# Score planes by level for the four chunks of a head, copied under constant masks, in the mixer of a two-layer encoder trunk

## The reference

```python
def chunk_gated_linear_attention(q, k, v, log_g):
    '''Per head: S_t = diag(exp(log_g_t)) S_{t-1} + k_t v_t^T,  o_t = S_t^T q_t.'''
    ...
    a_diag = jnp.einsum('bhcitsd,bhcisd->bhcits', q[..., :, None, :] * decay_diag, k)
    ...
    a_off = jnp.einsum('bhcitjd,bhcjsd->bhcitjs', qo, ko) * before[:, None, :, None]
    a_full = (a_off + a_diag[..., :, :, None, :] * eye).reshape(B, H, NC, CHUNK, CHUNK)
    o_intra = jnp.einsum('bhcts,bhcsv->bhctv', a_full, vc)
    ...
    o_inter = jnp.einsum('bhctd,bhcdv->bhctv', qc * jnp.exp(bc), s_prev)
    o = (o_intra + o_inter).transpose(0, 2, 3, 1, 4).reshape(B, T, H, DV)
```

## Time and profile before

| | |
|---|---|
| median of 3 runs | 1338.24 us (1330.84 to 1340.97) |
| profiled execution | 1322.33 us |
| its span, first to last instruction | 1320.6 us |
| PE busy | 1258.5 us (95%) |
| DVE busy | 719.9 us (55%) |
| ACT busy | 521.7 us (40%) |
| mean granted clock of TensorE | 0.984 |

### The profile page before, as it was taken

How to read it: one execution, slowest core, us unless ns; L and a number is a source line. 1 busy time by engine, 2 the same in 40 slices (tenths; PEclk the granted TensorE clock), 3 DMA queues, 4 the chain that set the end, 5 groups by cost and what they waited for, 6 DMA issues and landing times.

```text
span 1320.6 us, 16222 instructions
## 1 busy us (share of the span) xinstructions
PE 1258.5 (95%) x5981; PEld 1015.6 (77%) x5981; DVE 719.9 (55%) x1054; ACT 521.7 (40%) x1003; POOL 103.2 (8%) x108
## 2 busy tenths in 40 slices
PE   5899999888999999999999999999999999999997
PEld 3678787676798888888888786656798888888886
DVE  6558888877565344443447246563554343443444
ACT  4543544442553232242435673331553232332332
POOL 2221112210055000000000000000000000000000
PEclk7999999989999999999999999999999999999999
DMA  4321121111433332323222232000332322333321
GB/s 115 105 72 48 33 65 49 53 44 49 159 105 108 95 100 96 96 95 95 96 96 81 64 84 69 32 33 16 96 96 96 96 96 97 96 101 99 100 82 64
DMA packets 94866, 107.96 MB, mean 82 GB/s; under 512 B 15281, under 2 KB 56338, under 8 KB 94802
## 3 DMA queue, kind: packets, MB, share of 16 engines
q1 hardware_dynamic: 93618, 102.64, 25.1%
q0 software_dynamic: 1184, 4.46, 1.0%
HBM read 104.98 MB, written 2.10 MB: 81 GB/s over the span
## 4 chain that ended last, share of the span: by engine, by line
PE 86%; DVE 6%; ACT 4%; issue 2%; DMA 1%; POOL 0%; DVEq 0%; SPq 0%; ACTq 0%
PE bank L1339 24%; PE bank L1341 24%; PE bank L1340 24%; PE pp L1461 2%; PE pp L1705 1%; PE pp L1704 1%; PE po L1722 1%; DVE tmp L1120 1%; DVE a_sb L1123 1%; PE pp L1378 1%; PE pp L1458 1%; ACT w_hi L445 1%; PE pp L1340 0%; PE pp L1341 0%; PE pp L1339 0%
## 5 line engine op out<-in xcount | busy, mean ns | idle before, releaser
L1339 PE MATMUL bank<-h_lo,w_hi 128*128 128x512 f32 (+3 forms) x568 | 221.3, 390 | 9.7 <-DVE h_lo L984 5.8
L1340 PE MATMUL bank<-h_hi,w_lo 128*128 128x512 f32 (+3 forms) x568 | 217.9, 384 | 0.0
L1341 PE MATMUL bank<-h_hi,w_hi 128*128 128x512 f32 (+3 forms) x568 | 217.8, 383 | 0.0
L1339 PEld LDWEIGHTS bank<-h_lo,w_hi 128*128 128x128 f32 (+1 forms) x568 | 107.0, 188 | 35.6 <-issue 15.2
L1339 PE MATMUL bank<-wx,a_hi 128*128 128x512 f32 x320 | 126.7, 396 | 5.3 <-DVE wx L455 5.3
L1203 DVE TENSOR_TENSOR tmp<-sq,bank 128x512 f32<-128x512 f32 x64 | 44.0, 688 | 156.3 <-ACT sq L838 156.3
L1341 PE MATMUL bank<-wx,a_hi 128*128 128x512 f32 x320 | 125.2, 391 | 0.0
L1340 PE MATMUL bank<-wx,a_lo 128*128 128x512 f32 x320 | 125.2, 391 | 0.0
L1341 PEld LDWEIGHTS bank<-h_hi,w_hi 128*128 128x128 f32 (+1 forms) x568 | 107.1, 189 | 21.6 <-issue 0.6
L1340 PEld LDWEIGHTS bank<-h_hi,w_lo 128*128 128x128 f32 (+1 forms) x568 | 107.2, 189 | 20.7 <-issue 1.0
L1339 PE MATMUL bank<-w_lo,a_hi 128*128 128x512 f32 x304 | 119.9, 394 | 2.6 <-DVE a_lo L1099 1.4
(11 more groups left out here) (277 smaller groups left out, 2124.3 us busy)
## 6 DMA issues: line engine op xcount, KB each, us to landing
stage<-in_mlp_w SPq DMA_DIRECT2D x128, 512.0 KB, 3.6
stage<-in_ev_w_in SPq DMA_DIRECT2D x28, 512.0 KB, 3.7
stage<-in_ev_w_out SPq DMA_DIRECT2D x8, 512.0 KB, 3.6
stage<-in_od_w_out SPq DMA_DIRECT2D x8, 512.0 KB, 3.5
stage<-in_od_w_in SPq DMA_DIRECT2D x10, 256.0 KB, 3.0
x_tok<-in_x SPq DMA_DIRECT2D x4, 512.0 KB, 5.3
gbc<-in_norm_gains POOLq DMA_DIRECT2D x4, 512.0 KB, 4.1
xr<-in_x POOLq DMA_DIRECT2D x1, 2048.0 KB, 9.2
```

Source lines behind the costliest of these rows:

```text
L1339: nc.tensor.matmul(dst, wh, xl_, start=first, stop=False)
L1340: nc.tensor.matmul(dst, wl, xh, start=False, stop=False)
L1341: return nc.tensor.matmul(dst, wh, xh, start=False, stop=last)
```

## The change

A head's work is now cut by plane and not by chunk. `STEPS` makes four steps of a head: planes 0 and 1, 2 and 3, 4 and 5, and 6. For each plane PE writes the scores of all four chunks side by side into one bank of 512 columns, in a ring of four banks (`planes`). DVE copies each plane under its mask (`copy_predicated`: where the mask is not zero the element is written, elsewhere the target keeps what it has) into the head's score buffer for all four chunks, one of two (`a_bufs`: all of `a_sb`, and half of `tmp`). The masks are disjoint and the same for every head, so the buffers are cleared once, and each head overwrites the same elements. The mask of plane 0 was all ones, over a region that was zero but for its blocks; it now is one on the blocks of levels 0 and 1 alone. The four outputs of a head are issued together, two long slots after its last step. The slots themselves, and the number of steps in each, stay as they were.

```diff
+STEPS = [(0, 1), (2, 3), (4, 5), (6,)]
...
-            pending = [pending[1], groups]
+            pending = [pending[1], [(o, c) for o, step in groups if step == len(STEPS) - 1 for c in range(NT)]]
...
+        planes, a_bufs = quad, [a_sb[:, :, :], tmp[:, 0, :].rearrange("p (c t) -> p c t", c=NT)]
...
-            ch.link(nc.gpsimd.memset(masks[:, 0, :], 1.0))
+            for r, c in ((slice(0, 64), slice(64, 128)), (slice(0, 32), slice(32, 64)), (slice(64, 96), slice(96, 128))):
+                ch.link(nc.gpsimd.memset(masks[r, 0, c], 1.0))
...
-            for b in range(2):
-                nc.vector.memset(pp[b][:, 0, :], 0.0).then_inc(p_zero, 1)
+            nc.vector.memset(pp[0][:, 0:4, :], 0.0).then_inc(p_zero, 1)
...
-            def group(o, c):
-                idx = o * NT + c
-                pm = tmp[:, :, :].rearrange("p a t -> p (a t)")[:, 0:PAIRS * P]
-                dve.wait_ge(p_done, idx + 1)
-                if idx >= 1:
-                    dve.wait_ge(a_ready, idx)
-                nc.vector.tensor_tensor(pm, pp[idx % 2][:, 0:PAIRS, :].rearrange("p l t -> p (l t)"),
-                                        masks[:, :, :].rearrange("p l t -> p (l t)"), ALU.mult).then_inc(p_read, 1)
-                dve.wait_ge(p_read, idx + 1)
-                nc.vector.tensor_reduce(a_sb[:, idx % 4, :], pm.rearrange("p (l t) -> p t l", l=PAIRS),
-                                        AX_X, ALU.add).then_inc(a_ready, 1)
-                if c == 2 and FIRST[PACK_OF[o]] == o:
+            def group(o, step):
+                a = a_bufs[o % 2]
+                if step == 0 and o < 2:
+                    nc.vector.memset(a, 0.0).then_inc(a_zero, 1)
+                    dve.wait_ge(a_zero, o + 1)
+                elif step == 0:
+                    dve.wait_ge(o_done, o - 1)
+                for plane in STEPS[step]:
+                    n = o * PAIRS + plane
+                    dve.wait_ge(p_done, n + 1)
+                    if plane:
+                        dve.wait_ge(a_ready, n)
+                    mask = masks[:, plane:plane + 1, :].to_broadcast([P, NT, P])
+                    nc.vector.copy_predicated(a, mask.bitcast(I32), planes[n % 4]).then_inc(a_ready, 1)
+                if step == 2 and FIRST[PACK_OF[o]] == o:
                     update_state(PACK_OF[o])
...
+            def pairs(o, step):
+                p, r = PACK_OF[o], head_rows(o)
+                if step == 0:
+                    pe.wait_ge(xl_ready, (p + 1) * (LEVELS + 2))
+                for plane in STEPS[step]:
+                    n = o * PAIRS + plane
+                    if n == 0:
+                        pe.wait_ge(p_zero, 1)
+                    elif n >= 4:
+                        pe.wait_ge(a_ready, n - 3)
+                    for c in range(NT):
+                        dst, s = planes[n % 4][:, c, :], slice(c * P, (c + 1) * P)
+                        if plane == 0:
+                            ...
+                        elif plane < PAIRS - 1:
+                            x_ = xls[p % 2][r, plane + 1, s]
+                            ins = nc.tensor.matmul(dst, x_, x_, start=True, stop=True)
+                        else:
+                            ins = nc.tensor.matmul(dst, ks[p % 3][r, s], qs[p % 3][r, s], start=True, stop=True)
+                    ins.then_inc(p_done, 1)
...
-                pe.wait_ge(a_ready, idx + 1)
-                ins = nc.tensor.matmul(po[:, s], vbuf[:, o % 4, s], a_sb[:, idx % 4, :], start=True, stop=(c == 0))
+                pe.wait_ge(a_ready, (o + 1) * PAIRS)
+                ins = nc.tensor.matmul(po[:, s], vbuf[:, o % 4, s], a_bufs[o % 2][:, c, :], start=True, stop=(c == 0))
```

More of the change, by code:

```diff
@@ L593, in load_gain @@
                 pool.dma_start(gbc[:, :], norm_gains[layer, n].partition_broadcast(P)).then_inc(gbc_in, 16)
-            pool.wait_ge(a_ready, 8 * NT)
+            pool.wait_ge(a_ready, 8 * PAIRS)
             load_gain(0)
@@ L731, in evacuate @@
                 if what in ("q", "k") and i >= 3:
-                    act.wait_ge(p_done, NT * FIRST[i - 2])
+                    act.wait_ge(p_done, PAIRS * FIRST[i - 2])
                 if what == "f":
@@ L1030, in decayed @@
                 if lv == 0 and p >= 2:
-                    dve.wait_ge(p_done, NT * FIRST[p - 1])
+                    dve.wait_ge(p_done, PAIRS * FIRST[p - 1])
                 dve.wait_ge(e_ready, done + 2 if lv <= LEVELS else done + 1)
@@ L1407, in out_head @@
                     if idx == 0:
-                        pe.wait_ge(p_read, 8 * NT - 1) if j == 0 else pe.wait_ge(prob_exp, 4 * MLA_HEADS)
+                        pe.wait_ge(a_ready, 8 * PAIRS) if j == 0 else pe.wait_ge(prob_exp, 4 * MLA_HEADS)
                 if t == 0 or idx == KD - 1:
@@ L1446, in head_rows @@
                 return slice(first, first + w_)
-            def pairs(o, c):
-                p, idx, r, s = PACK_OF[o], o * NT + c, head_rows(o), slice(c * P, (c + 1) * P)
-                pe.wait_ge(xl_ready, (p + 1) * (LEVELS + 2))
-                if idx >= 2:
-                    pe.wait_ge(p_read, idx - 1)
-                else:
-                    pe.wait_ge(p_zero, idx + 1)
-                for lv in range(2):
-                    L = 64 >> lv
-                    for b in range(0, P, 2 * L):
-                        nc.tensor.matmul(pp[idx % 2][b:b + L, 0, b + L:b + 2 * L], xls[p % 2][r, lv, c * P + b:c * P + b + L],
-                                         xls[p % 2][r, lv, c * P + b + L:c * P + b + 2 * L], start=True, stop=True)
-                for lv in range(2, LEVELS):
-                    nc.tensor.matmul(pp[idx % 2][:, lv - 1, :], xls[p % 2][r, lv, s], xls[p % 2][r, lv, s],
-                                     start=True, stop=True)
-                nc.tensor.matmul(pp[idx % 2][:, PAIRS - 1, :], ks[p % 3][r, s], qs[p % 3][r, s], start=True,
-                                 stop=True).then_inc(p_done, 1)
+            def pairs(o, step):
[11 more added lines that the diff above has]
+                        if plane == 0:
+                            for lv in range(2):
+                                L = 64 >> lv
+                                for b in range(0, P, 2 * L):
+                                    left = xls[p % 2][r, lv, c * P + b:c * P + b + L]
+                                    right = xls[p % 2][r, lv, c * P + b + L:c * P + b + 2 * L]
+                                    ins = nc.tensor.matmul(dst[b:b + L, b + L:b + 2 * L], left, right, start=True, stop=True)
+                        elif plane < PAIRS - 1:
[4 more added lines that the diff above has]
+                    ins.then_inc(p_done, 1)
@@ L1466, in outputs @@
             def outputs(o, c):
-                p, idx, r, s = PACK_OF[o], o * NT + c, head_rows(o), slice(c * P, (c + 1) * P)
+                p, r, s = PACK_OF[o], head_rows(o), slice(c * P, (c + 1) * P)
                 if c == 0:
```

2 lines of the change are left out of this document (1 added, 1 removed).

## The result

| | before | after |
|---|---|---|
| median, runs of this comparison | 1334.54 us (1323.12 to 1340.97, 4 runs) | 1312.39 us (1305.08 to 1314.34, 4 runs) |
| profiled execution, its span | 1322.33, 1320.6 us | 1312.53, 1310.8 us |
| mean granted clock in it | 0.984 | 0.980 |
| PE, DVE busy | 1258.5, 719.9 us | 1259.0, 672.9 us |

The ratio measured is 0.9865, 95% interval 0.9822 to 0.9909: faster by a little over 1%, where 1324 us, 1.1% less, was forecast. The medians of four runs above are 22 us apart, but the four runs before lie 18 us from end to end. So the difference came out as forecast.

The account below looks back on a forecast made before the run. TensorE was taken to bound the kernel, mixer edits counting through its idle time and clock. 12.7 us of idle time plus 1.7 us of clock, 14.4 us off the 1338.24 us median, gave 1324 us; range 1311 to 1340 us.

Parts of the forecast that it names:

- PE sets the end, and only its gaps count: Whole kernel: TensorE is the bound; a mixer edit is worth its change in PE's idle time (22.0 us) and clock.
- Work taken off DVE is worth nothing by itself: Mixer: VectorE loses 52 us of 202, but this alone was to bring no time.
- comes from where the outputs stand: Mixer: most of the 14.4 us gain was credited to the outputs' new place, not to VectorE's relief.
- five gaps at outputs: PE waits of 1.80, 4.01, 1.04, 2.52 and 1.70 us in the mixer, all to go by issuing outputs later.
- Rival 1: Mixer: VectorE's lateness is behind all gaps; all 21.65 us and clock falls go, 25.4 us, 1313 us; chance 0.12.
- ScalarE's chain: Ahead of key transposes and chunk states: rinv work without idle time, 6.73 us from clamp to rinv; it was to stay.
- the 2.21 us that should have stayed: PE's gap at 215.03 us: chunk states wait for rinv on ScalarE, nothing of DVE in it; no gain claimed.
- rival 2: Mixer: gaps move, half of 12.7 us returns as waits for rinv or misc; 6 us less, 1332 us; chance 0.15.
- I cost this at nothing: TensorE's score matmuls: same number and shapes in another order, 0 us but for the clock.
- The fall at 300 us: Granted clock of 0.72 in 298 to 304 us after the 4.01 us gap; was to go with it, 1.7 us.
- rival 3: Runs of plane 0: four to eight clock falls of 1.7 us give back 7 to 14 us, 1331 to 1338 us; chance 0.12.
- Nothing in the trace to tell why: Base: the median of 1338.24 us stood 15.9 us above the profiled execution, unexplained; the gain was taken from the median.

Follow-up runs that it names:

- e8: Kernel before with VectorE's load taken down: sum over masked planes left out, one 128x128 copy in its place; 1312.86 us, ratio 0.9898.
- e1: Kernel before with only the four outputs of a head issued together, two slots after its last group; 1324.55 us, ratio 0.998.
- e2: Changed kernel with 72 further VectorE minima of 128x512 behind its copies, so VectorE's load is as before; 1327.51 us, ratio 1.0008.
- e9: Kernel before with a head's outputs issued together and the sum over masked planes replaced by one copy; 1313.14 us, ratio 0.9905.
- e5: The changed kernel measured again, unaltered, on another chip against the kernel before; 1311.34 us, ratio 0.9876.
- second batch: Runs on one chip of the kernel before (11 runs, median 1325.77 us) together with e5 to e8.
- e7: Changed kernel with ScalarE's rinv steps first in their slot and plane 0's small matmuls sorted by tile shape; 1290.49 us, ratio 0.9722.
- e6: Changed kernel with ScalarE's two rinv steps moved ahead of the evacuation, decays and cast in their slot; 1299.76 us, ratio 0.9789.
- e4: Changed kernel with plane 0's small matmuls sorted by shape, halves of all four chunks first, then quarters; 1302.27 us, ratio 0.9805.

## Why the prediction came out, and where its steps failed

- **Right: PE sets the end, and only its gaps count.** 383 to 700 us has 317.00 us of PE again.
- **Failed: "Work taken off DVE is worth nothing by itself", and with it that most of the gain "comes from where the outputs stand".** The relief alone is worth 12.9 us (e8), the place alone 0.3 us (e1), and with DVE's load put back nothing is left (e2). Each of the five gaps at outputs had been put down to position ("whatever DVE's speed"), since PE stood there one slot after DVE was given the work. But DVE was up to a whole slot late (8.6 us at the chunk states above), and its lateness made these gaps: four of them go and the fifth falls from 4.01 to 1.04 us when DVE alone is relieved. Rival 1 had the mechanism right for all but ScalarE's chain.
- **The gaps: right where named, but two were missed.** The 6.08 and 0.69 us and the outputs without any came as forecast; the 2.21 us that should have stayed became 2.61. I followed state to the outputs and not to the other reader of `misc`, though the order shows the sum of squares waiting for `state_ready`: 1.64 us, and 1.45 us behind it. Idle time fell by 9.2 and not by 12.7 us; that much of rival 2 came.
- **Mis-sized: TensorE's order, "I cost this at nothing".** By plane, the small matmuls follow each other and the large too, 0.2 to 0.4 us a head in the rows above, 2 to 3 us for eight. e9, which has the relief and the place but the old order, has a product of span and clock of 1289.4, the changed kernel 1285.4 us. That is 4 us, by medians from two batches, and no more than an indication by itself.
- **The clock: wrong in its places, near in sum, and not for the reason given.** The fall at 300 us stayed, with a gap still ahead of it. New ones came at 136 and 163 us with no gap ahead (rival 3's kind), both while PE was in the scores of a head with 64 rows, begun at 132.45 and 160.14; and one at 214.5, at the gap of 2.61 us, where the 2.21 us before had brought none. The places are not fixed: e5, the same kernel, has no fall at 136. In the profiled execution (1 - 0.980) x 1310.8 = 26.2 us are lost against (1 - 0.984) x 1320.6 = 21.1 us. By the medians of the second batch it is no loss but a gain: 0.979 before, 0.981 after, where 1.7 us were forecast and (1 - 0.979) x 1324.0 - (1 - 0.981) x 1309.6 = 2.9 us came, by the median spans. That figure is good to 2 or 3 us at best, since the median clock of the kernel before went from 0.977 to 0.980 between batches. So the forecast's 1.7 us came near for no reason that it gave.
- **The base.** "Nothing in the trace to tell why" the median stood 15.9 us above the profiled execution: in the second batch the runs before had times up to 1336.96 us, clocks of 0.970 to 0.982, and products of 1294.2 to 1298.2 us. The clock differs from run to run, the work hardly does. The profiled execution, at 0.984, was a good one. Over all 57 runs of the kernel before its median is 1326.8 us, over ten runs of the changed one 1312.3: the 1338.24 us of three runs was some 11 us high, and by itself put the forecast of 1324 us that much too high.
- **The sizes.** The copy took 735 ns, 0.69 forecast; DVE in the window 158 us and not 150: 2.5 us of this is the copies, and the rest goes with PE being further on at 331 us, the low part of head 6 at 319.69 and not 328.33.

So the second batch's 14.4 us are, by the products, 10.8 us of gaps and matmuls, by the clock 2.9, and the rounding of medians. The forecast had the same 14.4 us with 3.5 us too much in gaps, 2 to 4 us too little in matmuls and 1 too little in the clock. That these errors cancelled is luck.

## What to carry to other kernels

When an engine off the critical path is late by a slot, one lateness shows at many waits, and each of them can look like a matter of where its instruction stands; move the instruction, as e1 did, and the wait can go to the next reader of the same buffer. Relieve the late engine first, then look at the order of the engines that feed the gaps left: the same line on ScalarE was worth nothing before the relief and 11.6 us after it. Sort small matmuls by tile shape: it was worth some 9 us here.

## What the runs showed of the hardware

- A predicated copy of 128x512 float32, PSUM to SBUF under an int32 mask in SBUF, takes 735 ns, 1.44 ns an element, near the two-input add of the same size (688).
- Between float32 matmuls a change of tile shape costs PE: 24 records of 64 and 32 columns in 1.75 us, sorted in 0.97 us. An alternation of 128 and 64 rows seems to cost it as well. The outputs of the changed kernel, for a head with 64 rows and one with 128 (timeline of PE):

```profile
122.32 0.49 PE L1486 MATMUL po<-a_sb,vbuf 128*128 128x128 f32 x2
122.73 0.48 PE L1489 MATMUL po<-qe,state 64*128 64x128 f32 x2
...
238.96 0.39 PE L1489 MATMUL po<-qe,state 128*128 128x128 f32 x2
239.18 0.39 PE L1486 MATMUL po<-a_sb,vbuf 128*128 128x128 f32 x2
```

  The next piece comes 0.41 us later in the first and 0.22 us later in the second, for two records each, with the clock at 1.00 in both. No run varies this alone.
- The spread of this kernel's runs is mostly the granted clock of TensorE: over the 53 runs before in the three batches it goes from 0.966 to 0.986, while the product of span and clock stays within 1293.4 to 1299.8 us. The kernel with few gaps and sorted shapes (e7) had 0.987 to 0.991, and against e5 (1 - 0.981) x 1309.6 - (1 - 0.9905) x 1288.8 = 12.6 of its 20.9 us are clock (median spans). Which of the two steadies it is open: e6, with the fewest gaps, had 0.9855, and e4, with as many gaps as the changed kernel, 0.986.
